# The values of fifteen heads: turned in blocks on VectorE, stored, read back, and multiplied after the slot's projections

## The reference

```
# layer 0, differential heads
q_lat, kv_lat, kpe_raw, dq, dk, dv = split(h @ w_in)
dv_all = dv, or concat(cache_diff_v, dv) for the sample
attn   = softmax(map 0) - lam * softmax(map 1)
b_out  = attn @ dv_all
# layer 1, sparse attention
q, k, v, q_idx, k_idx, w_idx = split(h @ w_in)
out    = softmax(logits over the selected keys) @ v_all
# returned: y_prompt, y_sample and, for both groups, ckv, kpe,
# diff_k, diff_v (8 heads x 128), dsa_k, dsa_v (8 x 128), kidx
```

## Time and profile before

| | before |
|---|---|
| median of 3 runs | 1643.68 us (1642.51 to 1647.01) |
| profiled execution | 1643.9 us |
| its span, first to last instruction | 1642.1 us |
| mean granted TensorE clock | 0.997 |
| busy share: TensorE, its weight loads | 98%, 95% |
| busy share: VectorE, ScalarE, GpSimd | 73%, 55%, 55% |
| DMA over the span | 145.50 MB, 89 GB/s |

### The profile page before, as it was taken

One profiled execution on the slowest core, in us unless ns is written; L12 is line 12 of the kernel. 1 busy time (PEld: TensorE's weight loads), 2 busy tenths in 40 slices (PEclk: granted clock), 3 DMA queues, 4 the chain that ended last, 5 costly groups with the idle time before them and its releaser, 6 DMA issues.

```text
span 1642.1 us, 32437 instructions
## 1 busy us (share of the span) xinstructions
PE 1612.4 (98%) x12028; PEld 1563.2 (95%) x12028; DVE 1202.8 (73%) x2233; ACT 902.5 (55%) x1776; POOL 903.1 (55%) x703
## 2 busy tenths in 40 slices
PE   9999999999999999999999999999999999999998
PEld 8989999999999999999999999899999999999997
DVE  5666655656656799889897789634357998898977
ACT  4365545454546665565565445644367655655654
POOL 4453445364544067677575547664450676775754
PEclk9999999999999999999999999999999999999999
DMA  6221223343422223423323332344242233233232
GB/s 189 81 64 53 67 78 86 77 108 77 112 75 68 65 78 92 115 71 111 97 84 90 89 81 70 92 120 110 64 110 60 78 94 112 74 107 98 84 91 71
DMA packets 283008, 145.50 MB, mean 89 GB/s; under 512 B 60591, under 2 KB 273261, under 8 KB 282853
## 3 DMA queue, kind: packets, MB, share of 16 engines
q1 hardware_dynamic: 278392, 136.27, 30.1%
q0 software_dynamic: 3616, 6.92, 1.6%
q10 hardware_dynamic: 844, 0.24, 0.1%
HBM read 130.69 MB, written 15.32 MB: 89 GB/s over the span
## 4 chain that ended last, share of the span: by engine, by line
PE 81%; DVE 11%; ACT 3%; issue 3%; POOL 1%; DMA 0%; POOLq 0%; ACTq 0%; DVEq 0%
PE ACC L1444 29%; PE ACC L1883 11%; PE ACC L1884 11%; PE ACC L1885 11%; PE ACC L1724 2%; PE S L1699 2%; PE S L1885 2%; PE S L1883 2%; PE S L1884 2%; DVE SCO L3137 2%; DVE TOP L3134 1%; PE T L1444 1%; ACT PR L2335 1%; PE T L1712 1%; PE S L1673 1%
## 5 line engine op out<-in xcount | busy, mean ns | idle before, releaser
L3645 POOL TENSOR_TENSOR WL<-RAW,WH 128x1024 fp32r<-128x1024 f32 (+3 forms) x89 | 187.8, 2114 | 147.2 <-ACT WH L2210 147.0
L1444 PE MATMUL ACC<-XGh,WH 128*128 128x288 f32 (+1 forms) x1008 | 227.6, 307 | 6.3 <-DVE XGl L2828 1.8
L1444 PE MATMUL ACC<-XGh,WL 128*128 128x288 f32 (+1 forms) x1008 | 215.3, 295 | 0.0
L1444 PE MATMUL ACC<-XGl,WH 128*128 128x288 f32 (+1 forms) x1008 | 215.3, 295 | 0.0
L1883 PE MATMUL ACC<-TB,WH 128*128 128x288 f32 x640 | 188.5, 295 | 1.4 <-DVE TB L3355 1.4
L1885 PE MATMUL ACC<-TB,WL 128*128 128x288 f32 x640 | 188.6, 295 | 0.0
L1884 PE MATMUL ACC<-TB,WH 128*128 128x288 f32 x640 | 188.3, 294 | 0.0
L2493 ACT ACTIVATE TC<-ACC 128x288 f32<-128x288 f32 x192 | 79.0, 411 | 167.7 <-PE ACC L1885 167.0
L1444 PEld LDWEIGHTS ACC<-XGh,WH 128*128 128x128 f32 (+1 forms) x1008 | 159.0, 188 | 11.4 <-issue 4.0
L1444 PEld LDWEIGHTS ACC<-XGh,WL 128*128 128x128 f32 (+1 forms) x1008 | 161.6, 188 | 0.0
L1444 PEld LDWEIGHTS ACC<-XGl,WH 128*128 128x128 f32 (+1 forms) x1008 | 161.3, 187 | 0.0
(11 more groups left out here) (517 smaller groups left out, 5244.2 us busy)
## 6 DMA issues: line engine op xcount, KB each, us to landing
RAW<-in_w_gate_dram SPq DMA_DIRECT2D x44, 512.0 KB, 3.9
RAW<-in_w_up_dram SPq DMA_DIRECT2D x44, 512.0 KB, 5.0
RAW<-in_w_down_dram SPq DMA_DIRECT2D x48, 384.0 KB, 3.8
RAW<-in_w_in_even_dram SPq DMA_DIRECT2D x29, 512.0 KB, 5.2
RAW<-in_w_in_odd_dram SPq DMA_DIRECT2D x28, 512.0 KB, 4.6
RAW<-in_w_out_even_dram SPq DMA_DIRECT2D x16, 512.0 KB, 4.2
RAW<-in_w_down_dram SPq DMA_DIRECT2D x16, 256.0 KB, 2.9
RAW<-in_w_out_odd_dram SPq DMA_DIRECT2D x8, 512.0 KB, 5.1
```

The lines of the kernel that those rows point to most:

```text
L1444: ins = pe.matmul(out[0:m, 512 * b:512 * b + width], left, right[:, b * width:(b + 1) * width], start=(first and part == 0), stop=(last an ...
L3645: pool.tensor_tensor(WL[slot][:, 0:n], RAW[slot][:, 0:n], WH[slot][:, 0:n].bitcast(F32), ALU.subtract).then_inc(w_lo_pool, 1)
```

## The change

`blockwise(g)` is true for fifteen heads: 8 to 15 and 17 to 23. For these:
- The five transposes on TensorE and the two copies on VectorE go, with their entries in `tr`.
- VectorE turns the raw values in slot 0 with one instruction (`turn_values`), as it turns the keys. The turned blocks go to a new tile `VT`, which lies over `RSTDQ`. The turn waits for the projection's emptying and for the landing of the stores of the head before.
- SP stores `VT` with eight DMAs right behind the eight of the keys, in place of the wait for `VF` and two stores.
- At the end of its `attention(h)`, behind the weight loads of slots 4 to 7, SP waits until the stores have landed and until the split of the values of head `h - 1` is done, and reads the values back from the output into `VF` by two DMAs (`load_values`). The job "v" waits for these (`vf_in`).
- TensorE runs the product of head `h - 1` behind `prepare` in slot 1, where `values_late(h)` is true: heads 9 to 15 and 17 to 23. In 15, 22 and 23 there is no projection in the slot.

Head 16 and the mla heads keep the old way. The semaphore counts of stores (`value_stores`) follow.

```diff
@@ -146,6 +146,23 @@
 
 
     return h - 1 if h % 2 and kind_of(h) == "dsa" else None
+
+
+def blockwise(g):
+
+
+    return kind_of(g) != "mla" and g != 16
+
+
+def value_stores(g):
+
+
+    return 16 * sum(2 * QUADRANTS if blockwise(i) else 2 for i in range(8, g))
+
+
+def value_loads(g):
+
+    return 16 * 2 * sum(blockwise(i) for i in range(8, g))
 
 
 def q_job_slot(g):
@@ -391,8 +408,9 @@
             if (h, s) == (17, 0):
                 tr.add("p", 16, QT)
             if s == 1:
-                tr.add("v", h)
-                tr.add("v5", h)
+                if not blockwise(h):
+                    tr.add("v", h)
+                    tr.add("v5", h)
                 if h % 16:
                     group("pv", h - 1, use=SHORT)
             if s == first_output_slot(h) and p is not None and kind_of(p) == "mla":
@@ -775,6 +793,8 @@
         shared = cursor[0]
 
         RSTDQ = sb("RSTDQ", [P, NT])
+        (VT,), e = overlay(shared, ("VT", [P, NT // SQUARE, SQUARE], F32))
+        assert e <= cursor[0]
         arena = cursor[0]
         PTh, PTl = sb("PTh", [P, QT, SEQ], F32R), sb("PTl", [P, QT, SEQ], F32R)
 
@@ -892,7 +912,7 @@
         corners = sem("corners")
         bias_in, kc_in, kc_pool, vc_in = [sem(f"bias_in{i}") for i in range(2)], sem("kc_in"), sem("kc_pool"), sem("vc_in")
         kf_out, vf_out, lat_out, kif_out, y_out = (sem(n) for n in ("kf_out", "vf_out", "lat_out", "kif_out", "y_out"))
-        keys_made = sem("keys_made")
+        keys_made, vals_made, vf_in = sem("keys_made"), sem("vals_made"), sem("vf_in")
         chain = sem("dve_chain")
 
         y_made = sem("y_made")
@@ -1131,10 +1151,26 @@
                     tokens = outs[dst + name][:, c].rearrange("(b t) (q d) -> q t b d", t=SQUARE, d=SQUARE)
                     for q in range(QUADRANTS):
                         sp.dma_start(tokens[q], KF[q * SQUARE:(q + 1) * SQUARE, b0:b1, :]).then_inc(kf_out, 16)
+                dst = ("diff_v", "dsa_v")[kind_of(g) == "dsa"]
+                if blockwise(g):
+                    sp.wait_ge(vals_made, value_loads(g) // 32 + 1)
+                    for name, b0, b1 in (("_prompt", 0, SEQ // SQUARE), ("_sample", SEQ // SQUARE, NT // SQUARE)):
+                        tokens = outs[dst + name][:, c].rearrange("(b t) (q d) -> q t b d", t=SQUARE, d=SQUARE)
+                        for q in range(QUADRANTS):
+                            sp.dma_start(tokens[q], VT[q * SQUARE:(q + 1) * SQUARE, b0:b1, :]).then_inc(vf_out, 16)
+                    return
                 sp.wait_ge(t_free, tr.made("v5", g))
-                dst = ("diff_v", "dsa_v")[kind_of(g) == "dsa"]
                 sp.dma_start(outs[dst + "_prompt"][:, c].rearrange("(t p) d -> p t d", p=P), VF[:, 0:QT, :]).then_inc(vf_out, 16)
                 sp.dma_start(outs[dst + "_sample"][:, c], VF[0:DEC, QT, :]).then_inc(vf_out, 16)
+
+            def load_values(g):
+
+                sp.wait_ge(vf_out, value_stores(g + 1))
+                sp.wait_ge(job_lo, jobs.made("v", g - 1))
+                dst = ("diff_v", "dsa_v")[kind_of(g) == "dsa"]
+                c = slice((g % HEADS) * HD, (g % HEADS + 1) * HD)
+                sp.dma_start(VF[:, 0:QT, :], outs[dst + "_prompt"][:, c].rearrange("(t p) d -> p t d", p=P)).then_inc(vf_in, 16)
+                sp.dma_start(VF[0:DEC, QT, :], outs[dst + "_sample"][:, c]).then_inc(vf_in, 16)
 
             def load_next(*place):
 
@@ -1156,6 +1192,8 @@
                     if s == 4 and kind_of(h) != "mla":
                         store_keys(h)
                     load_next("slot", h, s)
+                if blockwise(h):
+                    load_values(h)
 
             def load_pair(layer, j):
                 if is_gate(j):
@@ -1225,7 +1263,7 @@
 
             sp.wait_ge(lat_out, 16 * 4)
             sp.wait_ge(kf_out, stored_keys(16))
-            sp.wait_ge(vf_out, 16 * 2 * 16)
+            sp.wait_ge(vf_out, value_stores(len(ALL_HEADS)))
             sp.wait_ge(kif_out, 16 * 2)
             sp.wait_ge(y_out, 16 * TOK_TILES)
 
@@ -1282,6 +1320,8 @@
                 return y_made, Y_MADE[w]
             if w in ("q", "k"):
                 return acc_free, acc.made(w, g)
+            if w == "v" and blockwise(g):
+                return vf_in, value_loads(g + 1)
             if w == "v":
                 return t_free, tr.made("v5", g)
             if w == "o":
@@ -1637,10 +1677,7 @@
 
             def values_to_tokens(h):
                 out = rotate_to_tokens(("v", h))
-                if h == 17:
-                    pe.wait_ge(y_made, Y_MADE["v"])
-                else:
-                    pe.wait_ge(acc_free, acc.made("v", h))
+                pe.wait_ge(acc_free, acc.made("v", h))
                 for t in range(QT):
                     ins = pe.transpose(out[:, t * P:(t + 1) * P], raw_values(h)[:, t * P:(t + 1) * P], IDN[:, :])
                 ins.then_inc(t_done, 1)
@@ -1702,6 +1739,11 @@
                                 pe.matmul(out[0:r, cols], mask_left, mask_right, start=False, stop=False)
                     ins.then_inc(s_done, 1)
 
+            def values_late(h):
+
+                c = share(h, 1)
+                return h > 8 and blockwise(h) and (c is None or c[3] < c[4])
+
             def turn_probs(h, t):
 
                 out = rotate_to_tokens(("p", h, t))
@@ -1803,9 +1845,10 @@
                         output_tile(*out_tile(h, s))
                     if 2 <= s < 2 + TOK_TILES and (h, s) != (16, 6):
                         turn_probs(h, s - 2)
+                    if s == 1 and not blockwise(h):
+                        values_to_tokens(h)
                     if s == 1:
-                        values_to_tokens(h)
-                        if h % 16:
+                        if h % 16 and not values_late(h):
                             weighted_values(h - 1)
                     if s == 3 and h in (9, 11, 13):
                         subnorm_sum(h - 1)
@@ -1820,6 +1863,8 @@
                             prepare(*c[:2], c[2] + 2, c[3])
                     elif c and not share_first(h, s):
                         prepare(*c[:4])
+                    if s == 1 and values_late(h):
+                        weighted_values(h - 1)
                     if (h, s) == (16, 4):
                         cached_keys_turned(x)
                     if s == 6:
@@ -2440,7 +2485,7 @@
             def take_first_values():
 
                 act.wait_ge(t_done, tr.made("v", 16))
-                act.wait_ge(vf_out, 16 * 2 * 8)
+                act.wait_ge(vf_out, value_stores(16))
                 act.wait_ge(t_free, tr.made("kc", 16))
                 act.activation(VF[:, 0:QT, :], T[tr.at("v", 16) % 2][:, :].rearrange("p (t d) -> p t d", t=QT),
                                ACT.Copy).then_inc(t_free, 1)
@@ -3024,12 +3069,20 @@
             def stored_before(g):
                 return g - 8
 
+            def turn_values(g):
+
+                if g == 17:
+                    dve.wait_ge(y_made, Y_MADE["v"])
+                else:
+                    dve.wait_ge(acc_free, acc.made("v", g))
+                if g > 8:
+                    dve.wait_ge(vf_out, value_stores(g))
+                dve.transpose(VT[:, :, :].rearrange("p b d -> p (b d)"), raw_values(g)[:, 0:NT]).then_inc(vals_made, 1)
+
             def take_values(h):
                 dve.wait_ge(t_done, tr.made("v", h))
                 if h:
                     dve.wait_ge(job_lo, jobs.made("v", h - 1))
-                if h > 8:
-                    dve.wait_ge(vf_out, 16 * 2 * stored_before(h))
                 dve.tensor_copy(VF[:, 0:QT, :], T[tr.at("v", h) % 2][:, :].rearrange("p (t d) -> p t d", t=QT)).then_inc(t_free, 1)
                 out = T[tr.at("v5", h) % 2]
                 dve.wait_ge(t_done, tr.made("v5", h))
@@ -3170,7 +3223,9 @@
                             take_keys(h)
                     if (h, s) == (17, 1):
                         take_keys(h)
-                    if s == 1 and h != 16:
+                    if s == 0 and blockwise(h):
+                        turn_values(h)
+                    if s == 1 and not blockwise(h) and h != 16:
                         take_values(h)
                     if keys_early(h, s):
                         write_projection(c[0], "k")
@@ -3444,7 +3499,7 @@
                 begin("g", layer, 0)
                 add_squares(norm - 1)
                 dve.wait_ge(kf_out, stored_keys(HEADS * (layer + 1)))
-                dve.wait_ge(vf_out, 16 * 2 * HEADS * (layer + 1))
+                dve.wait_ge(vf_out, value_stores(LAYER_HEADS[layer][-1] + 1))
                 token_sum(layer, 0)
                 rstd_mean(norm - 1)
                 token_sum(layer, 1)
```

## The result

The changed kernel takes 1650.31 us (median of 6 runs, 1648.26 to 1651.48) against 1643.10 us before (6 runs, 1641.94 to 1647.01): 7.2 us or 0.39% slower, ratio 1.0039, 95% interval 1.0026 to 1.0052. That lies inside the forecast range, near its slow end, but not where the forecast stood: the sum had 0.3 of the 7.2 us, and 0.39% is just outside the 0.3% that the forecast called no change.

A forecast was written before the change was run, and what follows sets the result against it. TensorE, busy nearly the whole span, was taken to bound the kernel. Transposes -6.0, late values in the last heads +4.8 and clock +1.5 gave +0.3 us on 1643.9, forecast 1644 us, range 1638 to 1651.

The forecast's parts named there:

- The saving (-6.0 us): Transposes leaving TensorE in slot 1: seven diff heads at 0.52 us and five dsa heads at 0.47 us.
- My fourth rival: Slot 1: TensorE would have waited there anyway, so only the end's 6.3 us stay, 1650 us; chance 0.05.
- The product's place (0 taken): Product behind slot 1's projections: VectorE late by at most 0.7 us, absorbed by the slot between; 0 to 9 us.
- The third rival: Full heads: the product's new place makes VectorE late on TensorE, 9 us more, 1653 us; chance 0.05.
- The turn and the stores in the full heads: VectorE's turns and the DRAM way, hidden outside heads 22 and 23: nothing taken; head 17's 0.6 us on ScalarE absorbed.
- Heads 22 and 23 (+4.8 us): Values read back late for ScalarE's split: 1.5 us in head 22, layer end 4.8 us later (1.8 to 9.4).
- The clock (+1.5 us): TensorE idle some 5 us in head 23, then at a granted clock of 0.50: 1.5 us lost (0 to 3.0).
- My second rival: Heads 22 and 23: stores drain slowly, ScalarE waits 9.4 us at head 23's split, 1648.8 to 1650.3 us; chance 0.13.
- the prediction's own signs: Heads 8 to 23: head 22 some 6 us earlier; wrong if TensorE's waits in full heads grow over a microsecond.

The follow-up runs named there:

- e2: Kernel before, with only the product moved behind slot 1's projections; values still turned by TensorE's transposes: 1650.69 us, ratio 1.0043.
- e1: Changed kernel with the product back in its old place, ahead of the slot's projections: 1645.62 us, ratio 1.0014.
- e8: Changed kernel with the product ahead of the projections and heads 22 and 23 back on TensorE's transposes: 1639.86 us, ratio 0.9982.
- e4: Changed kernel with the split of the values moved to slot 6 in heads 17, 22 and 23: 1646.58 us, ratio 1.0018.
- e5: As e8, but in heads 9, 11, 13, 19 and 21 the product stands behind the first of the slot's k tiles: 1638.41 us, ratio 0.9974.
- e3: Changed kernel with heads 22 and 23 back on TensorE's transposes, without reading values back: 1645.33 us, ratio 1.0015.
- e7: Changed kernel, all fifteen heads on the new way, with e5's product place and e4's later split: 1638.76 us, ratio 0.9972.
- e6: As e5, but heads 8 and 17 also take their values by TensorE's transposes: 1638.05 us, ratio 0.9970.

## Why the prediction was right in its range and wrong in its sum

**The saving (-6.0 us): right in ten of the twelve heads.** e2 has the product in the same place and keeps the transposes. Against it each of heads 9 to 14 and 18 to 21 is 0.46 to 0.56 us shorter in the changed kernel, from one first exponential to the next, as the rows said. Head 8 wins nothing (its row maxima are waited for 0.5 us longer), and head 17 loses 0.6 us.

In the product's old place it would have been wrong for odd heads: there e1 and e8 win almost nothing. Head 13 of the kernel before shows why:

```profile
440.62 0.76 DVE L2822 TENSOR_TENSOR X<-ACC,X 128x576 f32<-128x576 f32 x1 [1.03 <-PE ACC L1444]
```

This sum empties the accumulator pair that the product takes. It ends at 441.38, while the transposes run (440.99 to 441.51), so they covered the wait. My fourth rival named this ("TensorE would have waited at that place anyway") and I set it aside by the earlier trace rows, where no such wait stands, because the transposes themselves hid it.

**The product's place (0 taken): the step that failed.** "The buffers that they free are wanted one slot later, behind more projections." In heads 9, 11, 13, 19 and 21 the accumulator pair is wanted in the same slot, by the output tile that follows directly: five waits of 1.1 to 1.2 us (3.5 + 2.2 us). And the delay on VectorE, bounded at 0.7 us, is about that (in head 10 the scores end at 344.47, the row maxima begin at 345.16) and is not absorbed by the slot between: YQ's emptying hands 0.55 us of it to TensorE in heads 10, 12 and 14, +1.7 us in all. That is 7.4 us in waits. The bound of 9 us was in the text, and e2 measured 7.8 us by medians. The third rival was right about the mechanism's place, and in size it was closer than the value taken.

**The turn and the stores in the full heads: right, but for head 17.** Of the fifteen turns only head 17's waits, the copies that left paid for the others, and e1 finds no other new wait in heads 9 to 14. Head 17's wait was foreseen, with only "its own reciprocal and row maxima" behind it. But the turn of the keys stands behind it too, and the key stores wait for that:

```profile
1049.97 0.78 DVE L3080 STREAM_TRANSPOSE VT<-YV 128x576 f32<-128x576 f32 x1 [3.20 <-DMA out_dsa_v_sample_dram<-VF]
...
1051.04 0.77 DVE L3067 STREAM_TRANSPOSE KF<-YK 128x576 f32<-128x576 f32 x1
```

The keys' turn came at 1047.16 before; of the 3.9 us between, 1.9 are the head's own later start. So the key stores began at 1051.84 for the 1047.96 counted on. A load of weights, counted at nothing, took 1.84 us of issue behind the value stores, and the loads went out at 1062.53. ScalarE waited 3.84 us, where 0.6 were forecast. TensorE stood for 0.7 us in that head, which is in the sum below.

**Heads 22 and 23 (+4.8 us): right in mechanism, high in size.** Forecast 1.5 us in head 22, measured 1.08; forecast some 5 us at the split in head 23 with the 1.5 us handed on, measured 3.24 us and 1.0 us handed on. The sixteen stores took 8.16 us for the 9.2 counted; from the first load's issue at 1230.68 to the split at 1233.81 it was 3.1 us for the 2.5 counted. The queue was seen ("a nearly gapless ScalarE"), but not that moving one job in it would take away most of the cost: e4.

**The clock (+1.5 us): right.** The product's 512-column matmuls took 0.63 us for 0.39 us behind the gap, the whole product 0.9 us more and the tiles ahead of it 0.5 us. The Trainium skill (TensorE: Matmul & The Clock Gate, "What's actually happening") has it that "the default state is throttled, and activity releases the throttle". Head 23 agrees (0.66 over the 5 us behind its gap); behind e4's gap of 1.0 us the clock did not fall.

**Stores in small pieces.** My second rival had the stores drain slowly. Eight value stores took 4.0 us to issue in head 23, less than the 4.8 us of the keys in the earlier trace rows, and the sixteen of heads 22 and 23 landed 1.5 to 2.1 us after issue. The split in head 23 waited 3.24 us, where the rival wanted 9.4. The Trainium skill (DMA: Bandwidth & Descriptors, "Specifications") wants pieces of at least 512 B for full rate; no run here shows a price of the 128-B pieces.

The sum was forecast as -6.0 + 4.8 + 1.5 = +0.3. In the profiles it is -6.0 for the transposes (TensorE's busy time fell by 6.4); + 5.7 of new waits in heads 8 to 14 (BO 3.5, YQ 1.7, the row maxima of head 8 0.5); + 2.9 in heads 17 to 21 (BO 2.2, and 0.7 in head 17); + 5.1 in heads 22 and 23 with the clock in place of 6.3: 7.7, where the ledger has 7.9 from head 8 on. The two middle terms are the error.

So it is luck that the time lies inside the range. The range's upper end of +6.8 us was made of late values and the clock (9.4 + 3.0), which came to 5.1 together, and it held nothing for the place. It is luck too that rivals 2 and 4 gave 1649 to 1650 us: what they rest on did not happen. By the prediction's own signs it was wrong: TensorE's waits in the full heads grew by several microseconds, where one was the limit, and head 22 began 2.5 us later than before, not some 6 us sooner.

## What to carry to other kernels

Before moving a block of matmuls later, list what else uses its accumulator, in the same slot as well, and find the first user behind its new place: here the cover was in the order, and the move gave away more than the removed instructions were worth. An instruction that leaves an engine may have been the cover of a wait that no view shows; look for the release that ends just before its successor starts. When data come late, look first at what stands behind the waiting instruction in its queue: moving one job on ScalarE gave 3.7 us back without making the data any earlier.

## What was not expected of the hardware

Twice the clock fell in the middle of a run, behind small waits. In e1, head 8 (stretches as before, but columns of TensorE alone: length, busy (x), granted clock, DMA share, GB/s):

```profile
270.00:278.00 8.00, 6.27 (x44) 0.99 0.79 221
278.00:286.00 8.00, 8.00 (x54) 0.80 0.09 22
```

After a stretch with 6.27 of 8 us busy, the clock was 0.80 over the next, with 54 matmuls in it where the changed kernel had 64. e5 shows the same. The changed kernel, e3, e4, e7 and e8 have nearly the same waits there and no fall. Head 8 on the new way makes the waits longer (0.5 us before, 1.0 us after, for the row maxima); in e6, where it keeps the old way, six runs lie within 2.0 us, in e5 eleven within 4.9: a hint, no proof.

The tail of layer 0 holds the same matmuls in all these kernels, yet the granted clock there differs from one profiled execution to the next: from 535 to 550 us it was 1.00 in e1, e3, e7 and e8, 0.89 in the kernel before, the changed kernel, e2, e4 and e6, and 0.77 in e5. This moved everything behind it by up to 2.4 us (head 16 against head 15, as in the ledger: -1.7 us in e1, -0.1 us in the changed kernel, +0.7 us in e5), so a ledger from single profiles carries that much chance. What decides it was not tried.
